# First block's attention: 64-wide heads turned in pairs and 32-wide index heads in fours, scores from row groups into different banks

## The chip, the core and the metric

The kernel runs on one core of one Trainium2 chip. The metric is device time in microseconds of one execution. Five engines work from queues of their own: TensorE (PE; its weight loads are PEld), VectorE (DVE), ScalarE (ACT), GpSimd (POOL) and SyncE (SP), which issues nearly all DMAs. They meet at semaphores only.

## The reference

Two transformer blocks one after the other, batch 1, 256 tokens, width 1024, each of depth 2. The change is in the mixer of the first block, of which this is what matters:

```python
u = x @ w_in                       # 3400 columns, split:
a_cq, a_ckv, a_kpe, b_q, b_k, b_v, b_qi, b_ki, b_wi, c_qkv = split(u)
# a: 8 heads, keys 96 wide (64 + 32 rotary), values 64 wide
s = einsum('bqhd,bkhd->bhqk', q, k) * 96 ** -0.5; s = where(causal, s, -1e30)
o_a = softmax(s) @ v
# b: sparse attention. 8 index heads of 32 share one key; 4 heads of 64 share one key and value
rel = relu(einsum('bqhd,bsd->bqhs', rope(qi), rope(ki)))
score = where(causal, einsum('bqhs,bqh->bqs', rel, wi) * scale, -1e30)
sel = top_k(score, 64)             # o_b: softmax over the selected keys only
# c: 3 x 4 dilated-window heads of 64 with keys and values of their own,
#    joined by the softmax of their log-sum-exps
o = concat([o_a, o_b, o_c]) @ w_o
```

After it come a residual with layer norm and a mixture of experts (top 2 of 8 in one of 4 groups). The second block has a GLA mixer and an SSD mixer.

## The kernel before

`block1` runs the first block's two layers as a loop of two passes over all engines. Tokens lie on partitions in two tiles of 128 (`TT` = 2, index t); t = 1 attends to 256 keys, t = 0 to 128. A pass has the input projection (`project`, L604) into `U`, the latents' projections into `QM`, `KM` and `VM` (`dense`, L501), the indexer, the attention loop, the output projection, the router and the experts.

*Turns.* Heads lie along the free axis, and a score product contracts over the head's width, which must lie on partitions. So `turn` (L494) transposes each head's 128 tokens by a product with the identity into a PSUM bank, four heads to a bank, and ScalarE copies the bank (`copy`, L847) to `QT`, `KTt`, `QIT` or `KIT`. A 64-wide head fills partitions 0 to 63 only, a 32-wide one 0 to 31.

*Indexer* (the prefix of the attention). 18 turns (`qiT`, `kiT`), five copies, 16 products (L780) of 32 rows into six banks (`rel`), six copies with Relu to `REL0` (t = 0) and `REL` (t = 1), from which VectorE sums the index scores (`index_sums`, L1282) and later picks the top 64 (`index_best`, MAX8 and MATCH_REPLACE8).

*Attention loop.* Six groups g of four heads: 0 and 1 are the 96-wide ones, 2 to 4 the dilated, 5 the sparse one. With the two token tiles that makes twelve units, u = 2g + t. In turn u TensorE does, in this order: the turns of the next group (even u only, `group_turns`), the turns of the probabilities of u (`prob_turns`), the scores of unit u + 2 (`scores`, L551), one chunk of the second block's conditioning product (`ada_chunk`, L586: 32 columns of weights in each of four strips of the array) and the outputs of u (`outputs`, L573). VectorE softens unit u + 2 (`soften`: scale and mask L1116, maximum L1121, negation L1123), takes out the conditioning row (L1311) and the outputs, and between them does its index sums and top-k rounds in units 0 to 6. ScalarE copies the next group (`group_copies`), then the turned probabilities, then exponentiates unit u + 1 (L951). Units 0 and 1 are scored ahead of the loop.

*Banks.* PSUM's eight banks are handed out in rotation by `plan_block1`, in the order in which TensorE fills them: a fill waits until what stood in that bank, eight keys earlier, has been read (`claim`), a reader until it is filled (`filled`), and each write and each read is counted on a semaphore of its bank.

*Weights of the conditioning product.* SyncE loads chunk u, 2.1 MB in two halves, into one of three places (`HALVES`; one half lies in `QIT`, whose owner must be through: it waits for `("rel", 1, 3)`), chunk u + 3 when chunk u's product is done (L393). After the loop, at `o_ready`, it starts on the expert weights.

## Time and profile before

| | us |
|---|---|
| three timed runs | 2290.03, 2293.17 (median), 2296.86 |
| the profiled execution | 2284.75 |
| its span in the trace | 2283.2 |
| TensorE busy | 2053.2 (90%) |
| VectorE busy | 1204.2 (53%) |
| ScalarE busy | 726.9 (32%) |

Times in the trace are counted from the start of the span. Pass 0 of the layer loop has its indexer and attention loop at 114 to 209 us, pass 1 at 609 to 703. The page's chain of what ended last reaches back only to about 1028 us, the second block, so that the attention stage is read from timelines and windows. A TensorE row's duration includes the latency to PSUM of the last pass; the pace of a train of passes is read from start to start.

### The profile page before, as it was taken

The numbers are of one execution on the slowest core, as the hardware profiler recorded it, in microseconds if no ns is written. First come the engines' busy times: TensorE is split into PE (matmuls) and PEld (weight loads), VectorE is DVE, ScalarE is ACT, GpSimd is POOL, SyncE is SP. The second block draws the span as 40 slices with busy tenths as digits, with TensorE's granted clock in tenths as the row PEclk, the third lists the DMA queues.
The fourth block names the chain that finished last, engine by engine and source line by source line (L and its number), as shares of the span: only waits on it lengthen the run. The fifth ranks groups of instructions, "written<-read, shape, count | busy, mean of one in ns | idle before, by whom it ended". The sixth has DMA issues, their size and how long they took to land.

```text
span 2283.2 us, 32536 instructions
## 1 busy us (share of the span) xinstructions
PE 2053.2 (90%) x12086; PEld 1459.1 (64%) x12086; DVE 1204.2 (53%) x2131; ACT 726.9 (32%) x1317; POOL 167.6 (7%) x155
## 2 busy tenths in 40 slices
PE   6999888879999878868998999999979988998997
PEld 4777533326785423325886788888868776756896
DVE  3364411124373311136558586666666876845766
ACT  3453200114452100015334311111154436623332
POOL 2001100001002000005421100000000000000000
PEclk9999999999999989998999999999999998999999
DMA  7569699984589799961322232322212342333552
GB/s 219 186 235 342 218 409 408 396 320 140 192 286 313 280 357 396 397 261 48 111 74 74 93 129 74 111 107 78 82 65 75 130 145 95 130 106 138 211 185 99
DMA packets 151935, 440.38 MB, mean 193 GB/s; under 512 B 10368, under 2 KB 12848, under 8 KB 143456
## 3 DMA queue, kind: packets, MB, share of 16 engines
q1 hardware_dynamic: 142704, 412.72, 48.5%
q0 software_dynamic: 8352, 22.39, 3.4%
q10 hardware_dynamic: 720, 3.15, 0.3%
q8 instruction: 101, 1.65, 0.3%
q14 instruction: 58, 0.48, 0.1%
HBM read 534.52 MB, written 1.21 MB: 235 GB/s over the span
## 4 chain that ended last, share of the span: by engine, by line
PE 40%; DVE 6%; ACT 4%; DVEq 2%; issue 1%; DMA 1%; ACTq 0%; POOL 0%; SPq 0%; POOLq 0%
PE bank L2113 25%; PE bank L2204 11%; PE bank L2255 4%; DVE ARENA L3223 1%; ACT ARENA L2765 1%; PE bank L2118 1%; ACT UT L2536 0%; DVEq L2839 0%; ACTq L2539 0%; DVE XA L2840 0%; DVEq L3225 0%; DMA W<-in_ffn_w 0%; ACT ARENA L2758 0%; DVE WLO L3164 0%; ACT ARENA L2513 0%
## 5 line engine op out<-in xcount | busy, mean ns | idle before, releaser
L2549 ACT ACTIVATE WPH<-W 128x1024 fp32r<-128x1024 f32 x128 | 135.5, 1063 | 400.2 <-PE bank L2113 200.2
L2113 PE MATMUL bank<-UH,WPH 128*128 128x512 f32 (+1 forms) x512 | 174.2, 340 | 6.1 <-DVE UL L2847 2.7
L2113 PE MATMUL bank<-UL,WPH 128*128 128x512 f32 (+1 forms) x512 | 173.1, 338 | 0.0
L2113 PE MATMUL bank<-UH,WPL 128*128 128x512 f32 (+1 forms) x512 | 172.8, 338 | 0.0
L2885 DVE TENSOR_TENSOR WPL<-W,WPH 128x1024 fp32r<-128x1024 f32 x128 | 153.5, 1220 | 17.2 <-ACT WPH L2549 17.2
L2204 PE MATMUL bank<-WPH,MHH 128*128 128x512 f32 x384 | 149.8, 390 | 0.0
L2204 PE MATMUL bank<-WPL,MHH 128*128 128x512 f32 x384 | 149.5, 389 | 0.0
L2204 PE MATMUL bank<-WPH,MHL 128*128 128x512 f32 x384 | 149.4, 389 | 0.0
L1438 DVE TENSOR_TENSOR H<-SG,bank 128x256 f32<-128x256 f32 x24 | 10.1, 422 | 238.7 <-ACT SG L1014 238.7
L2113 PE MATMUL bank<-ARENA 128*128 128x64 f32 (+4 forms) x528 | 107.1, 363 | 19.4 <-DVEq L3263 7.8
L704 PE MATMUL bank<-WC,H 128*32 128x512 f32 x768 | 95.1, 639 | 28.6 <-DMA WC<-in_expert_w_down 24.1
L667 PE MATMUL bank<-W,XG 128*32 128x512 f32 x768 | 90.8, 614 | 24.9 <-DMA W<-in_expert_w_up 12.4
L2113 PEld LDWEIGHTS bank<-UH,WPH 128*128 128x128 f32 x512 | 97.8, 191 | 19.1 <-issue 3.6
L2113 PEld LDWEIGHTS bank<-ARENA 128*128 128x128 f32 (+1 forms) x528 | 81.9, 208 | 39.4 <-issue 19.3
L2113 PEld LDWEIGHTS bank<-UL,WPH 128*128 128x128 f32 x512 | 97.9, 191 | 10.4
L2113 PEld LDWEIGHTS bank<-UH,WPL 128*128 128x128 f32 x512 | 97.8, 191 | 10.2
L2113 PE MATMUL bank<-XHI,PHI 128*128 128x512 f32 (+2 forms) x264 | 100.0, 379 | 4.2 <-DVE XLO L2847 2.4
L667 PE MATMUL bank<-WA,XG 128*32 128x512 f32 x768 | 90.7, 614 | 13.0 <-DMA WA<-in_expert_w_up 13.0
L501 PE MATMUL bank<-W,XT 128*128 128x512 f32 x192 | 88.2, 619 | 11.7 <-DMA W<-in_w_in 7.0
L2113 PE MATMUL bank<-XHI,WLO 128*128 128x512 f32 (+2 forms) x264 | 97.2, 368 | 0.0
L2113 PE MATMUL bank<-XLO,PHI 128*128 128x512 f32 (+2 forms) x264 | 96.8, 367 | 0.0
L1014 ACT ACTIVATE SG<-bank 128x256 f32<-128x256 f32 x24 | 9.2, 384 | 263.9 <-issue 139.8
(449 smaller groups left out, 4249.9 us busy)
## 6 DMA issues: line engine op xcount, KB each, us to landing
WC<-in_expert_w_down SPq DMA_DIRECT2D x32, 2048.0 KB
W<-in_ffn_w SPq DMA_DIRECT2D x64, 1024.0 KB, 6.2
W<-in_ada_w SPq DMA_DIRECT2D x32, 1024.0 KB, 6.8
WA<-in_expert_w_gate SPq DMA_DIRECT2D x16, 2048.0 KB
WA<-in_expert_w_up SPq DMA_DIRECT2D x16, 2048.0 KB
W<-in_expert_w_gate SPq DMA_DIRECT2D x16, 2048.0 KB
W<-in_expert_w_up SPq DMA_DIRECT2D x16, 2048.0 KB
WC<-in_expert_w_down ACTq DMA_DIRECT2D x32, 1024.0 KB
```

Source lines behind the costliest of these rows:

```text
L501: last = nc.tensor.matmul(bank[r.bank(key)][:, 0:n], lhs[k], rhs[k], start=(k == 0), stop=(k == len(lhs) - 1))
L667: last = nc.tensor.matmul(bank[r.bank(key)][32 * g:32 * g + 32, :], xg[:, 4 * part + k, col:col + 32], WA[part][:, g, :, k, :], start=(par ...
L704: last = nc.tensor.matmul(bank[r.bank(key)][32 * g:32 * g + 32, :], H[i // MQ][:, f, 32 * g:32 * g + 32], WC[:, g, f, n * CHUNK:(n + 1) * ...
L1438: r.read_done(nc.vector.tensor_tensor(H[q // MQ][:], SG[q // MQ][:].rearrange("p (n f) -> p f n", f=2), bank[r.bank(key)][:, EH:2 * EH].re ...
L2113: return nc.tensor.matmul(bank[r.bank(key)][0:rows, cols[0]:cols[1]], lhs, rhs, start=start, stop=stop)
L2118: return nc.tensor.transpose(bank[r.bank(key)][0:m, j * P:j * P + k], src, ident[0:k, 0:k])
L2204: last = nc.tensor.matmul(bank[r.bank(key)][:, :], a, x[:, k, :], start=first and k == 0 and z == 0, stop=last_block and kp == 1 and k == ...
L2255: last = nc.tensor.matmul(bank[r.bank(key)][:, :], x[:, kk, tok], a[:, k, :], start=kp == 0 and k == 0 and z == 0, stop=kp == 3 and k == 1 ...
L2549: nc.scalar.activation(piece_view(WPH, q), piece_src(i, q), ACT.Copy).then_inc(hi_done, 1)
L2765: last = nc.scalar.activation(SEGD[:, jt, z, h, :], SEGD[:, jt, z, h, :], ACT.Exp, bias=NCUM[:, jt, col:col + 1])
L2885: nc.vector.tensor_tensor(piece_view(WPL, q), piece_src(i, q), piece_view(WPH, q).bitcast(F32), ALU.subtract).then_inc(lo_done, 1)
L3223: last = nc.vector.scalar_tensor_tensor(acc, src, CW[:, m, k:k + 1], acc, ALU.mult, ALU.add)
```

## The change

Sizes and sums stay; the layout of the turned heads, the order of the products and the banks change.

- A turn takes 128 columns: two neighbouring 64-wide heads, or four 32-wide ones. Head 2i + j of a group comes to lie on partition half j, slot i, and index head 4i + j on quarter j, slot i. Groups 2 to 4 have 8 turns in 2 banks instead of 16 in 4, group 5 6 in 2 instead of 10 in 3, the indexer 6 in 3 instead of 18 in 5. Groups 0 and 1 stay as they are.
- Where one key serves several heads it must lie on every half or quarter: a new tile `KREP` takes it, written by two VectorE copies and one more drain ahead of `rope_b`.
- A score product reads the rows of its half or quarter, and half j writes bank j of the unit. Both halves' first heads come first, then both second heads. So a unit at t = 0 has two banks instead of one, and the indexer's t = 0 four instead of two; ScalarE makes eight `rel` copies (four of 256 columns and four of 512) instead of six of 512, and VectorE softens t = 0 of groups 2 to 5 in two operations of two heads.
- `plan_block1` lists the new keys in the new order.

```diff
--- before.py
+++ after.py
@@ -135,6 +135,18 @@
         ins.then_inc(self.empty[self.at[key][0]], 1)
 
 
+def score_banks(u):
+
+    return 2 if u >= 4 else u % 2 + 1
+
+
+def score_heads(u, j):
+
+    if u >= 4:
+        return slice(j, 4, 2)
+    return slice(0, 4) if u % 2 == 0 else slice(2 * j, 2 * j + 2)
+
+
 def plan_block1(full, empty):
     r = Ring(full, empty)
     keys = []
@@ -144,16 +156,16 @@
     keys += [("cT", t) for t in range(TT)]
     keys += [("q", n, t) for n in range(2) for t in range(TT)]
     keys += [("kv", n, t) for n in range(2) for t in range(TT)]
-    keys += [("qiT", t, h) for t in range(TT) for h in range(2)] + [("kiT",)]
-    keys += [("rel", 0, j) for j in range(2)] + [("rel", 1, j) for j in range(4)]
+    keys += [("qiT", t) for t in range(TT)] + [("kiT",)]
+    keys += [("rel", t, j) for t in range(TT) for j in range(4)]
     for u in range(-2, 12):
         g2, t2 = divmod(u + 2, 2)
         if u < 10 and t2 == 0:
-            keys += [("qT", g2, 0), ("qT", g2, 1), ("kT", g2, 0)] + ([("kT", g2, 1)] if g2 < 5 else [])
+            keys += [(what, g2, i) for what in ("qT", "kT") for i in range(2 if g2 < 2 else 1)]
         if u >= 0:
             keys += [("pT", u, j) for j in range(u % 2 + 1)]
         if u < 10:
-            keys += [("s", u + 2, j) for j in range(t2 + 1)]
+            keys += [("s", u + 2, j) for j in range(score_banks(u + 2))]
         if u >= 0:
             keys += [("ada", u), ("o", u)]
     keys += [("oT", t, h) for t in range(TT) for h in range(2)]
@@ -237,7 +249,7 @@
             WDH0 = low.enter_context(nc.sbuf_tensor("WDH0", [P, KT, CHUNK], F32R))
         REL = sb("REL", [P, IDX_H, SEQ])
         QIT = sb("QIT", [P, IDX_H, SEQ])
-        KIT = sb("KIT", [IDX_D, SEQ])
+        KIT = sb("KIT", [P, SEQ])
         DMASK = sb("DMASK", [P, 3 * P])
 
         REL0 = PT[:].rearrange("p s h n -> p (s h n)")[:, 0:IDX_H * P].rearrange("p (h n) -> p h n", h=IDX_H)
@@ -251,6 +263,7 @@
         CQT = sb("CQT", [P, 3, SEQ])
         O = sb("O", [P, TT, D])
         AROW = sb("AROW", [P, 12, P])
+        KREP = sb("KREP", [P, TT, 2, P])
         place[0].close()
 
         place[0] = ctx
@@ -503,13 +516,15 @@
                 r.fill_done(last, key)
 
             def group_src(g, h, t, what):
-                if g < 2:
-                    hh = 4 * g + h
-                    return QM[:, t, hh * QH:(hh + 1) * QH] if what == "q" else KM[:, t, hh, :]
+                hh = 4 * g + h
+                return QM[:, t, hh * QH:(hh + 1) * QH] if what == "q" else KM[:, t, hh, :]
+
+            def pair_src(g, i, t, what):
+
                 if g < 5:
-                    c0 = C_DIL + ((g - 2) * 4 + h) * HD + (DIL_COLS if what == "k" else 0)
-                    return U[:, t, c0:c0 + HD]
-                return U[:, t, C_BQ + h * HD:C_BQ + (h + 1) * HD] if what == "q" else U[:, t, C_BK:C_BK + HD]
+                    c0 = C_DIL + (g - 2) * 4 * HD + i * P + (DIL_COLS if what == "k" else 0)
+                    return U[:, t, c0:c0 + P]
+                return U[:, t, C_BQ + i * P:C_BQ + (i + 1) * P] if what == "q" else KREP[:, t, 1, :]
 
             def values(g, h, k):
                 if g < 2:
@@ -525,32 +540,40 @@
                     r.read(pe, ("kv", 1, 1), l)
                 if g == 2:
                     pe.wait_ge(rope_c, l + 1)
-                for t in range(TT):
-                    turn(l, ("qT", g, t), [group_src(g, h, t, "q") for h in range(4)])
-                if g < 5:
+                if g < 2:
+                    for t in range(TT):
+                        turn(l, ("qT", g, t), [group_src(g, h, t, "q") for h in range(4)])
                     for t in range(TT):
                         turn(l, ("kT", g, t), [group_src(g, h, t, "k") for h in range(4)])
                 else:
-                    turn(l, ("kT", g, 0), [group_src(g, 0, t, "k") for t in range(TT)])
+                    turn(l, ("qT", g, 0), [pair_src(g, i, t, "q") for i in range(2) for t in range(TT)])
+                    turn(l, ("kT", g, 0), [pair_src(g, i, t, "k") for i in range(2 if g < 5 else 1) for t in range(TT)])
 
             def scores(l, u):
                 g, t = divmod(u, 2)
-                dd = QH if g < 2 else HD
-                r.read(pe, ("qT", g, 1), l)
-                r.read(pe, ("qT", g, 0), l)
-                r.read(pe, ("kT", g, 0), l)
-                if g < 5:
-                    r.read(pe, ("kT", g, 1), l)
-                n = (t + 1) * P
+                for what in ("qT", "kT"):
+                    for i in range(2 if g < 2 else 1):
+                        r.read(pe, (what, g, i), l)
+                n, tok = (t + 1) * P, slice(t * P, (t + 1) * P)
+                if g >= 2:
+                    for j in range(2):
+                        r.claim(pe, ("s", u, j), l)
+                    for i in range(2):
+                        for j in range(2):
+                            key, rows = ("s", u, j), slice(j * HD, (j + 1) * HD)
+                            last = nc.tensor.matmul(bank[r.bank(key)][:, i * n:(i + 1) * n], QT[rows, g % 2, i, tok],
+                                                    KTt[rows, g % 2, i if g < 5 else 0, 0:n], start=True, stop=True)
+                            if i == 1:
+                                r.fill_done(last, key)
+                    return
                 per = 4 if t == 0 else 2
                 for j in range(t + 1):
                     key = ("s", u, j)
                     r.claim(pe, key, l)
                     for i in range(per):
                         h = j * per + i
-                        last = nc.tensor.matmul(bank[r.bank(key)][:, i * n:(i + 1) * n],
-                                                QT[0:dd, g % 2, h, t * P:(t + 1) * P],
-                                                KTt[0:dd, g % 2, h if g < 5 else 0, 0:n], start=True, stop=True)
+                        last = nc.tensor.matmul(bank[r.bank(key)][:, i * n:(i + 1) * n], QT[0:QH, g % 2, h, tok],
+                                                KTt[0:QH, g % 2, h, 0:n], start=True, stop=True)
                     r.fill_done(last, key)
 
             def prob_turns(l, u):
@@ -763,23 +786,22 @@
 
                 pe.wait_ge(rope_b, l + 1)
                 for t in range(TT):
-                    for h in range(2):
-                        turn(l, ("qiT", t, h), [U[:, t, C_QI + (4 * h + j) * IDX_D:C_QI + (4 * h + j + 1) * IDX_D] for j in range(4)])
-                turn(l, ("kiT",), [U[:, t, C_KI:C_KI + IDX_D] for t in range(TT)])
+                    turn(l, ("qiT", t), [U[:, t, C_QI + i * P:C_QI + (i + 1) * P] for i in range(2)])
+                turn(l, ("kiT",), [KREP[:, t, 0, :] for t in range(TT)])
                 for t in range(TT):
-                    for h in range(2):
-                        r.read(pe, ("qiT", t, h), l)
+                    r.read(pe, ("qiT", t), l)
                 r.read(pe, ("kiT",), l)
                 for t in range(TT):
-                    n = (t + 1) * P
-                    per = 4 if t == 0 else 2
-                    for j in range(IDX_H // per):
-                        key = ("rel", t, j)
-                        r.claim(pe, key, l)
-                        for i in range(per):
-                            last = nc.tensor.matmul(bank[r.bank(key)][:, i * n:(i + 1) * n],
-                                                    QIT[0:IDX_D, j * per + i, t * P:(t + 1) * P], KIT[:, 0:n], start=True, stop=True)
-                        r.fill_done(last, key)
+                    n, tok = (t + 1) * P, slice(t * P, (t + 1) * P)
+                    for j in range(4):
+                        r.claim(pe, ("rel", t, j), l)
+                    for i in range(2):
+                        for j in range(4):
+                            key, quarter = ("rel", t, j), slice(j * IDX_D, (j + 1) * IDX_D)
+                            last = nc.tensor.matmul(bank[r.bank(key)][:, i * n:(i + 1) * n], QIT[quarter, i, tok], KIT[quarter, 0:n],
+                                                    start=True, stop=True)
+                            if i == 1:
+                                r.fill_done(last, key)
 
                 group_turns(l, 0)
                 scores(l, 0)
@@ -854,19 +876,17 @@
                              bank[r.bank(key)][:, :].rearrange("p (k n) -> p k n", k=4))
 
             def group_copies(l, g):
-                dd = QH if g < 2 else HD
                 for what, dst in (("qT", QT), ("kT", KTt)):
-                    for t in range(TT):
-                        key = (what, g, t)
-                        if key not in r.at:
-                            continue
-                        if g >= 2 and what == "qT" and t == 0:
+                    for i in range(2 if g < 2 else 1):
+                        key = (what, g, i)
+                        if g >= 2 and what == "qT":
                             r.filled(act, ("s", 2 * (g - 2) + 1, 1), l)
-                        if what == "kT" and g == 5:
-                            copy(l, key, dst[0:dd, g % 2, 0, :], bank[r.bank(key)][0:dd, 0:SEQ])
+                        if g < 2:
+                            copy(l, key, dst[0:QH, g % 2, :, i * P:(i + 1) * P],
+                                 bank[r.bank(key)][0:QH, :].rearrange("p (h n) -> p h n", h=4))
                         else:
-                            copy(l, key, dst[0:dd, g % 2, :, t * P:(t + 1) * P],
-                                 bank[r.bank(key)][0:dd, :].rearrange("p (h n) -> p h n", h=4))
+                            m = 1 if what == "kT" and g == 5 else 2
+                            copy(l, key, dst[:, g % 2, 0:m, :], bank[r.bank(key)][:, 0:m * SEQ].rearrange("p (i n) -> p i n", i=m))
 
             def gathered(l, j, half):
 
@@ -930,18 +950,15 @@
                         r.read_done(nc.scalar.activation(
                             VM[:, t, 256 * n:256 * n + 256].rearrange("p (h d) -> p h d", h=4), b[:, :, NOPE:], ACT.Copy), key)
                 for t in range(TT):
-                    for h in range(2):
-                        key = ("qiT", t, h)
-                        copy(l, key, QIT[0:IDX_D, 4 * h:4 * h + 4, t * P:(t + 1) * P],
-                             bank[r.bank(key)][0:IDX_D, :].rearrange("p (h n) -> p h n", h=4))
-                copy(l, ("kiT",), KIT[:], bank[r.bank(("kiT",))][0:IDX_D, 0:SEQ])
+                    key = ("qiT", t)
+                    copy(l, key, QIT[:, 0:2, t * P:(t + 1) * P], bank[r.bank(key)][:, 0:SEQ].rearrange("p (i n) -> p i n", i=2))
+                copy(l, ("kiT",), KIT[:], bank[r.bank(("kiT",))][:, 0:SEQ])
                 for t in range(TT):
                     n = (t + 1) * P
-                    per = 4 if t == 0 else 2
-                    for j in range(IDX_H // per):
+                    for j in range(4):
                         key = ("rel", t, j)
-                        copy(l, key, (REL0, REL)[t][:, j * per:(j + 1) * per, 0:n],
-                             bank[r.bank(key)][:, 0:per * n].rearrange("p (h n) -> p h n", h=per), ACT.Relu)
+                        copy(l, key, (REL0, REL)[t][:, j:IDX_H:4, 0:n],
+                             bank[r.bank(key)][:, 0:2 * n].rearrange("p (h n) -> p h n", h=2), ACT.Relu)
                 group_copies(l, 0)
 
                 def weights_of(u):
@@ -1105,16 +1122,16 @@
 
                 g, t = divmod(u, 2)
                 n = (t + 1) * P
-                per = 4 if t == 0 else 2
                 m0 = 0 if t == 0 else P
                 mask = (DMASK if g == 5 else MASK[:, (0, 0, 1, 2, 3)[g], :])[:, m0:m0 + n]
                 if u >= 3:
                     r.filled(v, ("pT", u - 3, (u - 3) % 2), l)
-                for j in range(t + 1):
+                per = 2 if score_banks(u) == 2 else 4
+                for j in range(score_banks(u)):
                     key = ("s", u, j)
                     r.filled(v, key, l)
                     r.read_done(nc.vector.scalar_tensor_tensor(
-                        PR[:, u % 3, j * per:(j + 1) * per, 0:n],
+                        PR[:, u % 3, score_heads(u, j), 0:n],
                         bank[r.bank(key)][:, 0:per * n].rearrange("p (h n) -> p h n", h=per),
                         (QH if g < 2 else HD) ** -0.5, bc(mask, 1, per), ALU.mult, ALU.add), key)
                 v.drain()
@@ -1257,6 +1274,9 @@
                 rope(U[:, :, C_QI:C_WI].rearrange("p t (h d) -> p t h d", d=IDX_D), 9, HALF_I, HALF_M + HALF_H)
                 nc.vector.tensor_scalar(U[:, :, C_WI:C_DIL], U[:, :, C_WI:C_DIL], IDX_D ** -0.5 * IDX_H ** -0.5, None, ALU.mult)
                 nc.vector.tensor_copy(KM[:, :, :, NOPE:QH], bc(U[:, :, C_KPE:C_KPE + ROPE], 2, MLA_H))
+                v.drain()
+                for i, (c0, dd) in enumerate(((C_KI, IDX_D), (C_BK, HD))):
+                    nc.vector.tensor_copy(KREP[:, :, i, :].rearrange("p t (m d) -> p t m d", d=dd), bc(U[:, :, c0:c0 + dd], 2, P // dd))
                 v.drain().then_inc(rope_b, 1)
                 for n in range(5, N_IN):
                     low_weights(n)
@@ -1275,10 +1295,9 @@
 
                 def index_sums(t, h0, h1):
                     sc, mask, n = index_span(t)
-                    per = 4 if t == 0 else 2
                     for h in range(h0, h1):
-                        if h % per == 0:
-                            r.read(v, ("rel", t, h // per), l)
+                        if h < 4:
+                            r.read(v, ("rel", t, h), l)
                         nc.vector.scalar_tensor_tensor(sc, (REL0, REL)[t][:, h, 0:n], U[:, t, C_WI + h:C_WI + h + 1],
                                                        mask if h == 0 else sc, ALU.mult, ALU.add)
                         v.drain()
```

## Rows read from the trace of the kernel before

**Rows 1.** The head of the page: span and number of instructions.
```profile
span 2283.2 us, 32536 instructions
```

**Rows 2.** Windows, pass 0: stretch, length, busy us (count) by engine, clock, DMA, GB/s.
```profile
117.00:129.00 12.00, 10.55 (x48) 8.58 (x48) 3.49 (x10) 6.72 (x13) 0.00 (x0) 0.72 0.68 239
...
145.00:165.00 20.00, 19.16 (x297) 17.38 (x300) 16.57 (x54) 11.61 (x36) 0.00 (x0) 1.00 0.94 343
```

**Rows 3.** Windows, pass 1, same columns.
```profile
617.00:629.00 12.00, 11.12 (x49) 9.20 (x48) 3.60 (x7) 6.89 (x17) 0.00 (x0) 0.58 0.27 88
```

**Rows 4.** TensorE, timeline, pass 0, prefix: start, lasting, engine, line, out<-in, shape, count.
```profile
114.85 2.13 PE L494 MATMUL bank<-ident,U 128*32 128x128 f32 x18
117.92 6.97 PE L780 MATMUL bank<-KIT,QIT 32*128 32x128 f32 x32 [0.95 <-ACT KIT L847]
...
129.36 2.86 PE L551 MATMUL bank<-KTt,QT 96*128 96x128 f32 x16 [0.88 <-ACT KTt L847]
...
137.00 1.96 PE L586 MATMUL bank<-W,cond 128*32 128x128 f32 x64
```

**Rows 5.** Timeline of all engines, pass 0, prefix: ScalarE's copies, same columns.
```profile
115.59 2.02 ACT L847 ACTIVATE QIT<-bank 32x512 f32<-32x512 f32 x4
...
117.50 0.38 ACT L847 ACTIVATE KIT<-bank 32x256 f32<-32x256 f32 x1
...
119.11 0.60 ACT L847 ACTIVATE PT<-bank 128x512 f32<-128x512 f32 x1 [1.24 <-PE bank L780]
...
120.01 0.60 ACT L847 ACTIVATE PT<-bank 128x512 f32<-128x512 f32 x1 [0.30 <-PE bank L780]
...
120.87 0.60 ACT L847 ACTIVATE REL<-bank 128x512 f32<-128x512 f32 x1 [0.27 <-PE bank L780]
121.74 0.60 ACT L847 ACTIVATE REL<-bank 128x512 f32<-128x512 f32 x1 [0.27 <-PE bank L780]
```

**Rows 6.** Timeline of TensorE, pass 0, loop, units 5 to 8.
```profile
166.21 1.04 PE L494 MATMUL bank<-ident,PR 128*128 128x128 f32 x8
...
172.82 1.91 PE L494 MATMUL bank<-ident,U 128*64 128x128 f32 x16
174.57 0.60 PE L494 MATMUL bank<-ident,PR 128*128 128x128 f32 x4
175.74 1.15 PE L551 MATMUL bank<-KTt,QT 64*128 64x128 f32 x8 [0.56 <-ACT KTt L847]
176.81 1.95 PE L586 MATMUL bank<-W,cond 128*32 128x128 f32 x64
178.70 1.10 PE L573 MATMUL bank<-U,PT 128*128 128x64 f32 x8
...
180.61 1.99 PE L551 MATMUL bank<-KTt,QT 64*128 64x256 f32 x8
182.53 1.08 PE L586 MATMUL bank<-XT,cond 128*32 128x128 f32 x32
```

**Rows 7.** Timeline of TensorE, pass 1, prefix.
```profile
612.27 6.39 PE L780 MATMUL bank<-KIT,QIT 32*128 32x128 f32 x32 [0.95 <-ACT KIT L847]
...
623.12 4.73 PE L551 MATMUL bank<-KTt,QT 96*128 96x128 f32 x16 [0.88 <-ACT KTt L847]
...
631.68 1.96 PE L586 MATMUL bank<-W,cond 128*32 128x128 f32 x64
```

**Rows 8.** Timeline of VectorE, pass 0, input projection.
```profile
84.82 4.64 DVE L1221 TENSOR_TENSOR WLO<-W,WDH 128x1024 fp32r<-128x1024 f32 x4 [3.69 <-ACT WDH L899]
```

**Rows 9.** Timeline of VectorE, pass 0, loop, softening of unit 5.
```profile
159.31 1.29 DVE L1116 SCALAR_TENSOR_TENSOR PR<-bank,MASK 128x512 f32<-128x512 f32 x2 [0.17 <-issue]
...
161.98 0.17 DVE L1123 TENSOR_SCALAR MX<-MX 128x4 f32<-128x4 f32 x1
```

**Rows 10.** Timeline of ScalarE, pass 0, loop: last exponential of unit 5.
```profile
164.01 0.51 ACT L951 ACTIVATE PR<-PR,MX 128x256 f32<-128x256 f32 x1
```

**Rows 11.** DMA of 130 to 208 in 40 equal slices: GB/s of each.
```profile
GB/s 0 0 0 0 8 150 399 353 346 398 398 129 255 411 383 310 406 371 57 312 405 348 338 406 303 47 367 401 313 382 404 267 208 382 360 325 393 400 327 390
```

## Prediction

> **What bounds the kernel now.** I read the page first [rows 1]: 2283.2 us of span, one core. The change touches only the attention stage of the first block, which runs once in each of two passes of the layer loop, so I went to the windows of that stage. In pass 0 [rows 2] TensorE is busy 10.55 of 12 us in the short prefix (117 to 129, clock 0.72, so part of it was granted 1.2 GHz and not 2.4) and about 19 of 20 us in the loop over twelve units (clock 1.00). VectorE is busy 16.57 of 20 us there and the DMA engines are at 0.94. In pass 1 [rows 3] the prefix has clock 0.58. So the loop is TensorE's, but VectorE and DMA stand close behind: a saving on TensorE is worth its size only until one of them comes last. Everything after the loop hangs on `o_ready` (SyncE waits for it before the expert weights, TensorE before the mixing product), so what the stage loses, the span loses one for one.
>
> **How products and turns are paced.** An fp32 product stands in the trace as two passes. Eight passes of 128 columns lie between the first two relevance copies, 120.01 - 119.11 = 0.90 us, 0.112 us a pass; four of 256 columns between the next two, 121.74 - 120.87 = 0.87, 0.217 us [rows 5]. These use 32 rows of the array and are no faster than others. Scores of a 64-wide group take 1.07 us at t = 0 (175.74 to 176.81) and 1.92 at t = 1 (180.61 to 182.53), 16 turns 1.75 (172.82 to 174.57), 0.109 each [rows 6]. 32 passes that go to four different 32-column strips last 1.08 from 182.53 with some 0.27 of latency at the end (0.29 by (b) below), 0.026 each [rows 6]: strips of columns do run side by side, four for one. Strips of rows are never used side by side in this trace, so the price of the new products has to be bounded: at best 0.112/2 and 0.217/2 a pass with 64 rows and a quarter of them with 32, at worst the paces above plus a change of strip, for which the difference between 8 x 0.112 = 0.90 and the 1.07 above (0.17 for a change in and one out, some 0.1 each) is the nearest row.
>
> There is a middle: the eight passes of L573, only 64 moving columns wide, last 1.10 from 178.70 with the same latency, (1.10 - 0.27) / 7 = 0.118 each [rows 6], as long as 128 columns. There the load of 128 weight columns sets the pace. If such loads into different strips queue up, passes of 128 columns gain nothing and those of 256 go from 0.217 to 0.112. I take the best case, since the column strips of the trace show loads as well as products of four strips overlapping; the others are rivals. The Trainium skill ("TensorE: Matmul & The Clock Gate", LDWEIGHTS) says that a load's time goes by its columns and not its rows: the trace agrees (L573), and by this rule alone the middle case would hold. Its Part 3 gives 3.07x for four row tiles at 512 columns; no row here shows it, and by that factor the best case would lose about a quarter of its gain in the index products.
>
> **Part 1, the prefix.** Before, in pass 0 [rows 4, 5]: turns from 114.85, ScalarE's four QIT copies from 115.59 (0.48 apart) and the KIT copy at 117.50, products from 117.92, first copy 119.11, scores from 129.36. After:
> (a) 6 turns for 18. ScalarE is free at 115.59, so the turns saved (12 x 0.109 = 1.3) are mostly hidden behind it; but it now makes two copies of 256 columns and KIT's (0.38 lasting, about 0.28 apart) and is through at 115.59 + 2 x 0.28 + 0.38 = 116.53. Products start at 116.57, 1.35 earlier.
> (b) Products: four passes in each strip of rows, 4 x 0.112 = 0.45 for t = 0 and 4 x 0.217 = 0.87 for t = 1, where they took 6.9 us to 124.83. First copy: 116.57 + 0.45 + 0.3 (latency, 119.11 - 117.92 - 0.90) + 0.1 = 117.4.
> (c) ScalarE now comes last: four copies of 256 columns, 0.28 apart (1.1; two of 512 before), four of 512, 0.5 apart (2.0), the four group copies, 3 x 0.49 + 0.59 (2.1): 117.4 + 5.2 = 122.6. The 16 turns of group 0, unchanged, end by 116.57 + 1.4 + 3.5 = 121.5 even at 1.2 GHz (twice 1.75), so they lie beside it. Scores from 122.65 against 129.36: 6.7 us. The same steps in pass 1, where 612.27 to 623.12 = 10.85 us lie between product and scores [rows 7], give 1.35 + 10.85 - 6.1 = 6.1.
> (d) The clock. From first scores to the first conditioning chunk it is 7.64 us in pass 0 at 2.4 GHz (129.36 to 137.00 [rows 4]) and 8.56 in pass 1, partly at 1.2 (623.12 to 631.68 [rows 7]). TensorE will stand idle more ahead of these scores, so I take pass 1's 8.56 for both (-0.9 in pass 0) and another 1.0 in each, between 0 and 3.6 (scores and 16 turns at half pace: 1.75 + 1.9 more).
> (e) VectorE's index sums (about 3.3 us) start with the first copy and end by 121.2, before it is wanted. The two KREP copies and the drain, about 0.8 us, fall into the 3.69 us in which VectorE waits for ScalarE before 84.82 [rows 8]: nothing; uncovered they would cost 0.8. SyncE waits for ("rel", 1, 3) with one load, issued earlier now: nothing.
> Prefix: 6.7 - 0.9 - 1.0 + 6.1 - 1.0 = 9.9 us for both passes.
>
> **Part 2, the loop, groups 2 to 5.** (f) Turns: 8 for 16 in groups 2 to 4, 6 for 10 in group 5. From the first turn to the scores it is 2.92 us (172.82 to 175.74 [rows 6]), because the scores wait for the last of four copies. With two: turned at 0.87 + 0.27, the second copy starts at 1.22, ends at 1.81, scores at 1.85: 1.05 each. Group 5, which has 4 turns and one copy fewer to save, about 0.45 (4 x 0.109 by the turns). (g) Scores: 4 x 0.112 = 0.45 at t = 0 and 4 x 0.217 = 0.87 at t = 1 saved, 5.3 for four groups. Together 3.6 + 5.3 = 8.9 a pass on TensorE's own count.
> (h) VectorE takes some back. Its queue holds mask, softmax and top-k rounds in program order; through units 3 and 4 it never waits for TensorE. Its last operation of softening unit 5 starts at 161.98 [rows 9], then ScalarE's exponentials, the last from 164.01, 0.51 long with a readout behind it [rows 10], then unit 5's turn on TensorE, at 166.21 [rows 6]. That turn can move to 164.65 at the earliest, 1.56 us, where TensorE would gain 1.05 x 2 + 0.45 x 2 + 0.87 = 3.9. So 2.3 are lost there; after it TensorE is last again (s7 0.87, turns 1.05, s8 0.45, s9 0.87, turns 0.45, s10 0.45, s11 0.87 = 5.0). Softening a t = 0 unit from two banks adds one operation's overhead, some 0.09. Net 1.56 + 5.0 - 0.1 = 6.5 a pass, 13.0 for both. The bank order makes ("s", u + 4, 1) wait for ("s", u + 3, 0) to be read; that read starts at 159.31 [rows 9], within the same bound.
>
> **Sum.** 9.9 + 13.0 = 22.9 us. Against the profiled execution's own 2284.75 that is 2261.9; that execution lies 8.4 below the median of the timed runs (2293.17), to which I apply the sum: 2270.3, taken as 2270.
>
> **Rivals.**
> *Loads queue (middle case).* 16 passes at t = 0 take 1.8 and the first copy comes at 118.1: prefix 0.6 less a pass. The loop keeps f, loses the 0.45s: 5.5 a pass. 8.5 + 11.1 = 19.6: 2273.5.
> *No overlap of row strips at all.* For it: nothing in the trace shows any. The turns and copies still go: prefix about 2.5 a pass after the clock, loop 1.56 + 1.05 + 0.45 = 3.1. 11 us: 2282. If each change of strip also costs the 0.1 above (3 to 7 in a unit's scores, 15 in the index products, some 3.9 a pass) it is 3 us: 2290.
> *The conditioning weights become the bound.* Nine chunks of 2.1 MB are loaded in the loop, each when the one three units earlier is used. In the slices they run at up to 411 GB/s, mostly 310 to 406 [rows 11], 5.3 us a chunk; TensorE uses one every 6.6 now, every 5.5 after. At the 343 GB/s of the window [rows 2] a chunk takes 6.1 and the last lands just as it is wanted; at 332, the mean of the slices from the first full one on [rows 11], it takes 6.3 and the last comes 1.5 us late, at 300 it takes 7.0 and comes 7 late. I take 3.5 a pass between them: 2277.
> *The clock falls in the loop (the slower side).* TensorE now waits for VectorE in places where it had none, and packed products are fewer. Against it: clock 1.00 with 64-row products and packed strips of columns. A stretch T at 1.2 GHz costs up to T/2; it decides beyond 46 us of the two loops' some 126. At half of them, 63 us: +31 - 23 = +8, 2301.
>
> **How the numbers follow.** Best case 0.50, queued loads 0.20, no overlap 0.10, with costly changes 0.05, DMA 0.08, clock 0.04, something larger than I count 0.03. Predicted is the likeliest, 2270. The range reaches up through "no overlap" (2282) with the spread of the runs, 2286, and down to 2257, where the clock costs nothing (2 + 0.9), VectorE's hold is half of mine (2) and the runs come out as the profiled one did (8.4). The bound of what this kernel's timing can tell from no change is 0.3%, 6.9 us: faster 0.88 (the first three, DMA and the larger, less 0.03 of the plain no-overlap case, whose 11 us are nearest to the bound), same 0.08 (those 0.03 and the costly changes), slower 0.04 (the clock).
>
> **What the changed profile would show.** First relevance copy about 2.6 us and not 4.3 after the first index turn; scores of group 0 about 6 us after the first index product (11 before). Passes of L780's line starting in fours (best), every 0.112 (queued) or as before (no overlap). Scores of groups 2 to 5 in some 0.6 and 1.05 us. VectorE busier in the loop, and TensorE waiting for ScalarE's exponentials before the turn of unit 5. I am wrong if the group-0 scores start less than 3 us earlier, if TensorE waits for `ada_w` loads, or if clock digits in the loop are under 1.

## The result, and the profile after

The changed kernel takes 2264.27 us (median of 6 runs, 2259.13 to 2268.83) against 2289.32 for the kernel before beside it (2280.28 to 2296.86). The ratio is 0.9895, 95% interval 0.988 to 0.9909: 1.05% or 25 us faster. The profiled execution is the 2259.13 one, with a span of 2257.6 against 2283.2 [rows 1].

```profile
span 2257.6 us, 32346 instructions
```

Windows of the same stretches as [rows 2, 3] (stretch, length, busy us and count of TensorE's products, its weight loads, VectorE, ScalarE, GpSimd, then clock, DMA share, GB/s):

```profile
117.00:129.00 12.00, 9.28 (x78) 7.91 (x79) 7.13 (x16) 8.81 (x23) 0.00 (x0) 0.86 0.70 259
145.00:165.00 20.00, 17.82 (x300) 15.62 (x295) 16.77 (x56) 9.12 (x31) 0.00 (x0) 1.00 0.98 341
...
597.00:609.00 12.00, 8.84 (x74) 7.59 (x75) 7.85 (x17) 8.87 (x23) 0.00 (x0) 0.86 0.74 263
```

In the prefix TensorE is no longer nearly full (9.28 of 12 us where it was 10.55) and its clock is better, not worse: 0.86 for 0.72 and 0.58. In the loop TensorE fell from 19.16 to 17.82 of 20 us: now it waits there. The clock stays 1.00.

TensorE in the prefix of pass 0, which answers to [rows 4] (start, lasting, engine, line, out<-in, shape, count, idle time before it and its releaser):

```profile
115.12 0.60 PE L507 MATMUL bank<-ident,U 128*128 128x128 f32 x4
115.56 0.38 PE L507 MATMUL bank<-ident,KREP 128*128 128x128 f32 x2
117.14 1.59 PE L801 MATMUL bank<-KIT,QIT 32*128 32x128 f32 x32 [1.20 <-ACT KIT L869]
118.66 1.08 PE L507 MATMUL bank<-ident,QM 128*96 128x128 f32 x8
119.57 1.04 PE L507 MATMUL bank<-ident,KM 128*96 128x128 f32 x8
123.19 4.52 PE L575 MATMUL bank<-KTt,QT 96*128 96x128 f32 x16 [2.58 <-ACT KTt L869]
```

The 32 passes of the index products last 1.59 us; they lasted 6.97 [rows 4]. Then TensorE is through with its turns at 120.6 and stands idle for 2.58 us until ScalarE has copied. ScalarE in the same stretch, which answers to [rows 5]:

```profile
115.86 0.67 ACT L869 ACTIVATE QIT<-bank 128x256 f32<-128x256 f32 x2
116.39 0.41 ACT L869 ACTIVATE KIT<-bank 128x256 f32<-128x256 f32 x1
117.85 1.21 ACT L869 ACTIVATE PT<-bank 128x256 f32<-128x256 f32 x4 [1.04 <-PE bank L801]
118.92 2.10 ACT L869 ACTIVATE REL<-bank 128x512 f32<-128x512 f32 x4
120.83 1.13 ACT L869 ACTIVATE QT<-bank 96x512 f32<-96x512 f32 x2
121.79 1.15 ACT L869 ACTIVATE KTt<-bank 96x512 f32<-96x512 f32 x2
```

From 117.85 to the end of the KTt copies ScalarE has no gap: it is the engine that comes last, as the forecast said.

TensorE in the loop of pass 0, units 4 to 8, which answers to [rows 6]:

```profile
142.52 0.71 PE L564 MATMUL bank<-KTt,QT 64*128 64x128 f32 x8 [0.38 <-ACT KTt L869]
143.17 1.08 PE L609 MATMUL bank<-W,cond 128*32 128x128 f32 x32
...
146.97 1.14 PE L564 MATMUL bank<-KTt,QT 64*128 64x256 f32 x8
148.03 1.96 PE L609 MATMUL bank<-W,cond 128*32 128x128 f32 x64
...
154.70 0.71 PE L564 MATMUL bank<-KTt,QT 64*128 64x128 f32 x8 [1.47 <-DVE PR L1133]
...
159.05 1.07 PE L507 MATMUL bank<-ident,PR 128*128 128x128 f32 x8 [0.72 <-ACT PR L968]
...
164.83 1.04 PE L507 MATMUL bank<-ident,U 128*128 128x128 f32 x8
...
166.62 0.71 PE L564 MATMUL bank<-KTt,QT 64*128 64x128 f32 x8 [0.30 <-ACT KTt L869]
```

Scores take 0.65 us at t = 0 (142.52 to 143.17) and 1.06 at t = 1 (146.97 to 148.03), where they took 1.07 and 1.92 [rows 6]. Two waits are new: the scores of unit 6 wait 1.47 us for VectorE to read unit 5's banks, and the turn of unit 5 waits 0.72 us for its exponentials. Pass 1 has the same two, 1.46 and 0.72.

The stage by its marks, in both kernels (each mark is the start of a group in TensorE's timeline; us):

| stretch | before, pass 0 / 1 | after, pass 0 / 1 | gained | forecast |
|---|---|---|---|---|
| first index turn to first index product | 3.08 / 3.08 | 2.02 / 2.02 | 1.06 + 1.06 | 1.35 + 1.35 |
| to group-0 scores | 11.43 / 10.85 | 6.06 / 6.05 | 5.37 + 4.80 | 5.35 + 4.75 |
| to first conditioning chunk | 7.65 / 8.56 | 8.23 / 8.17 | -0.58 + 0.39 | -1.9 - 1.0 |
| to the turn of O | 71.75 / 71.74 | 65.67 / 65.44 | 6.08 + 6.30 | 6.5 + 6.5 |
| sum | 93.91 / 94.23 | 81.97 / 81.68 | 24.5 | 22.9 |

Of the 25.6 us of the span 24.5 lie in this stage. The rest of the kernel varies by itself: from the turn of O in pass 0 to the first index turn in pass 1, of which the kernels here change nothing but the two KREP copies, it is 400.4 us before, 398.5 after, and 397.4 to 403.9 in others. So single spans say little about steps of 1 to 4 us. The marks of the prefix repeat to a few hundredths where the clock is the same, those of the loop mostly to 0.1 to 0.3 (65.38 to 65.67 in six passes of the same loop code), and below I read those first.

Part of the gain comes through the clock: the stage has 17.1 us at 1.2 GHz before (6.8 + 10.2) and 6.8 after (3.4 + 3.4). At half pace 17.1 us cost at most 8.5, and the 6.8 cost 1.1 (8.23 and 8.17 us from scores to first chunk, where it is 7.64 at 2.4 GHz). So at most some 7 of the 24.5 us came this way, an estimate. No run separates them.

### The profile page after: what moved, and what is told of

Same layout as the page of the kernel before. It is cut to its first block, busy times and chain, and to the rows that moved or that the text cites. A ratio compares the mean times of both kernels' runs of the same rounds, so it can differ in the third digit from the quotient of the medians.

```text
span 2257.6 us, 32346 instructions
## 1 busy us (share of the span) xinstructions
PE 2023.1 (90%) x12006; PEld 1433.2 (63%) x12006; DVE 1204.8 (53%) x2143; ACT 718.2 (32%) x1303; POOL 167.7 (7%) x155
## 4 chain that ended last, share of the span: by engine, by line
PE 40%; DVE 7%; ACT 4%; DVEq 2%; issue 1%; DMA 1%; ACTq 0%; POOL 0%; SPq 0%; POOLq 0%
PE bank L2132 25%; PE bank L2223 11%; PE bank L2274 4%; DVE ARENA L3242 1%; ACT ARENA L2784 1%; PE bank L2137 1%; DVEq L2858 0%; ACT UT L2555 0%; ACTq L2558 0%; DMA W<-in_ffn_w 0%; DVE XA L2859 0%; ACT ARENA L2777 0%; DVE WLO L3183 0%; DVEq L2913 0%; DVE MHL L2924 0%
```

## The experiments

**Do the strips overlap because the program interleaves them?** The passes of each strip were put together, instead of going from strip to strip:

```diff
-                    for i in range(2):
-                        for j in range(2):
+                    for j in range(2):
+                        for i in range(2):
...
-                    for i in range(2):
-                        for j in range(4):
+                    for j in range(4):
+                        for i in range(2):
```

> The changed kernel with the two product loops exchanged (strip outside, head inside), so that all passes of one strip of rows come before those of the next. Turns, copies, banks and numbers of instructions stay. Theory (passes in different strips run side by side, and this order is what lets them): scores go back from about 0.65 and 1.06 us to 1.05 and 1.9, the index products from 1.5 to some 5.3 us; group-0 scores 6.1 -> about 8 us after the first index product, 9.5 if the clock falls; in the loop nothing is lost before unit 5, where the hold of VectorE (2.2 us) covers 0.43 + 0.86 + 0.43, and 3.4 us a pass behind it. 10 to 14 us in all over the changed kernel, about 2276. Rival (wide turns and fewer copies bring nearly all, overlap little): at most 3 us over the changed kernel.

Measured: 2265.71 us, ratio 0.9899 (0.9872 to 0.9925), as the changed kernel. My expectation missed, and the trace says how:

```profile
116.66 1.71 PE L801 MATMUL bank<-KIT,QIT 32*128 32x128 f32 x32 [1.20 <-ACT KIT L869]
118.29 0.97 PE L507 MATMUL bank<-ident,QM 128*96 128x128 f32 x7
```

The 32 passes last 1.71 for 1.59. In the records of the single passes the first four start at 116.656, .669, .686 and .700, and the passes that signal the four banks, each the last of its strip at t = 0, start at 117.063, .106, .119 and .136. The signals themselves, which are events and not modelled ends, come 0.69, 0.75, 0.81 and 0.87 us after the first start. Had the strips been worked one after another, each bank would have been signalled 0.45 us (4 x 0.112) before the next; had passes only been held to start in their order, still some 0.34 (3 x 0.112). So a pass for another strip does not wait for the ones before it in the source. (The trace doesn't show in which order the compiled program holds them; that it kept the source's order is taken, not shown.) This kernel therefore did not take the overlap away and can't price it. The Trainium skill ("TensorE: Matmul & The Clock Gate", Part 3, The mechanism) says that MATMULs start strictly in the order of the program; the start times recorded here differ from that if the compiled program kept the source's order, and by the 0.34 us above a strict order would have made this kernel slower (an estimate).

**What is the overlap worth?** First attempt: the same order, and a drain of TensorE behind each strip (`pe.drain()` after the strip's last pass, 24 a pass of the layer loop), with a control that has as many drains at the same places in the kernel before, where nothing overlaps.

> The changed kernel with the passes of one strip of rows issued together and a drain of TensorE behind each strip (8 a pass in the index products, 16 in the scores of groups 2 to 5), so that no two strips can run side by side. Theory (strips of rows run beside each other whatever the program's order, and that is most of the gain of the new products): index products last 5.3 us or more and not 1.3, scores 0.9 to 1.1 at t = 0 and 1.8 to 2.0 at t = 1 where they are 0.72 and 1.14; of the 5.3 + 5.3 us of TensorE's time a pass that come back, some 1.8 in the prefix (ScalarE covers the rest) and 3.5 in the loop (the hold of unit 5 covers the rest) reach the end: 10.6 us for both passes over the changed kernel, and on top what the drains cost (0 to 0.27 each, 0 to 13 us; the control with the same drains in the kernel before says how much). Rival (the gain lies in fewer turns and copies, the overlap is worth little): no more over the changed kernel than the control is over the kernel before.

> Control: the kernel before with a drain of TensorE after every two products of the index products and of the scores of groups 2 to 5, as many drains at the same places as in the kernel with its strips kept apart. Nothing overlaps here in any case, so what it costs over the kernel before is the drains' own price: 48 drains in both passes, between 0 and 0.27 us each (the latency behind a last product), so 0 to 13 us; I take 0.1 each, 5 us.

Measured: strips kept apart 2301.73 us, ratio 1.0051 (1.0032 to 1.0069); the control 2307.22, ratio 1.0078 (1.0059 to 1.0097), both slower than the kernel before. The control missed its forecast of 5 us: it lost 18. In its loop 16 drains cost 5.35 us (77.10 for 71.75), 0.33 each and not 0.1, and in the prefix of pass 0 it had 13.7 us of 1.2 GHz, where the kernel before had 6.8. In the loop the two can be set against each other: 74.06 - 65.67 = 8.4 us a pass over the changed kernel less the control's 5.35 leaves 3.0 (3.2 in pass 1) against a forecast of 3.5, if a drain costs the same in both kernels. In the prefix they can't: with the strips apart the index products and the scores behind them lie in 17.1 and 20.5 us of 1.2 GHz. So the loop speaks for the overlap, and the prefix stayed open.

Second attempt, without drains: as many products, over all rows of the array (the heads are no longer kept apart, so the values are not the reference's).

```diff
-                            key, rows = ("s", u, j), slice(j * HD, (j + 1) * HD)
+                            key, rows = ("s", u, j), slice(0, P)
...
-                            key, quarter = ("rel", t, j), slice(j * IDX_D, (j + 1) * IDX_D)
+                            key, quarter = ("rel", t, j), slice(0, P)
```

> The changed kernel with its index products and the scores of groups 2 to 5 over all 128 rows of the array and not over a quarter or half of them: same turns, copies, banks, order and number of products, no drains, but no strips of rows (so the heads are not kept apart, and these products are not the reference's). Theory (strips of rows side by side are what makes the new products cheap): index products last 5.3 us (16 x 0.112 + 16 x 0.217) and not 1.22; ScalarE's copies then end later, and group-0 scores come some 8.2 us after the first index product and not 6.06 (+2.1); the loop becomes 3.5 us a pass longer (0.45 or 0.87 for each unit's scores, those of units 4 to 6 inside VectorE's hold); 11 us in all over the changed kernel, near 2275. Rival (what the kernel with drains lost came from drains and clock, strips are worth little): within 3 us of the changed kernel.

Measured: 2274.54 us, ratio 0.9932 (0.9904 to 0.9959); by the marks 88.02 + 86.39 = 174.4 us against 163.65, 10.8 more where 11 were expected.

```profile
117.12 5.48 PE L801 MATMUL bank<-KIT,QIT 128*128 128x128 f32 x32 [1.20 <-ACT KIT L869]
122.44 1.04 PE L507 MATMUL bank<-ident,QM 128*96 128x128 f32 x8
...
125.59 2.86 PE L575 MATMUL bank<-KTt,QT 96*128 96x128 f32 x16 [1.24 <-ACT KTt L869]
...
133.24 3.43 PE L609 MATMUL bank<-W,cond 128*32 128x128 f32 x64
```

From the first start to the last of the 32 index passes it is 5.10 us here and 1.22 in the changed kernel, a ratio of 4.2. That overstates it, because the last pass of each strip runs on behind the last start: up to the signal of the last bank it is 5.49 and 1.69 us, 3.3 times with the latency in both, and with one pass of 0.217 added to each it is 5.3 and 1.4, 3.7 times. The group-0 scores come 8.47 us after the first product and not 6.06 (8.2 expected). The loop is 68.26 in pass 1, 2.8 over the changed kernel; in pass 0 it is 69.89, of which 1.6 are the 3.4 us at 1.2 GHz from 133.5 on (the chunk at 133.24 lasts 3.43, and 1.96 at 2.4 GHz). So the overlap is worth some 10 of the 25 us, and the theory holds. The other 13.7 by the marks are turns, copies and the clock together. The Trainium skill ("TensorE: Matmul & The Clock Gate", Part 3, Measured speedup vs the span model) has 3.07x for four row tiles at 512 columns. Here, at 128 and 256 columns of fp32, it is 3.3x up to the last signal, a little above; the starts of the changed kernel come in fours some 0.11 and 0.22 us apart, which is the full gain in pace.

**How do the two parts share the gain?** Only the indexer's part of the change (its turns, copies, products, KREP and the sums' order) was put into the kernel before, groups 2 to 5 left as they were.

> The kernel before with the indexer's part of the change alone (6 turns, 16 products in four strips, 8 banks, KREP); groups 2 to 5 as before. Theory (the two parts add up, neither is hidden): group-0 scores 6.1 us after the first index product, the loop from first conditioning chunk to the turn of O 71.7 us as before; 11.5 to 13 us under the kernel before, about 2277. Rival (an earlier start is given back in the loop, by the conditioning weights or VectorE): the loop grows by some 3 us a pass and 5 to 7 us are left.

Measured: 2278.51 us, ratio 0.9958 (0.9943 to 0.9973). Turn to product 2.02, product to scores 6.06, as in the changed kernel, and the loop 71.75 in both passes, as before. In pass 1 scores to first chunk took 9.72 with 6.8 us at 1.2 GHz, so it has less than its full share; in pass 0, at 2.4 GHz, 7.64. By the marks 11.1 us are gained over both passes and by the times 9.1, where 11.5 to 13 were expected; the rival's longer loop did not come. The parts are independent: prefix one, loop the other.

**Does VectorE hold TensorE in the loop?** The top-k rounds were left out of the changed kernel and of the kernel before (group 5 then attends to other keys than in the reference):

```diff
-                    for _ in range(rounds):
+                    for _ in range(0):
```

> The changed kernel without the 16 top-k rounds of each pass (MAX8 and MATCH_REPLACE8 left out, so group 5 attends to other keys than the reference); VectorE has some 15 us a pass less to do in units 1 to 6. Theory (VectorE holds TensorE back by 2.2 us a pass at the scores of unit 6 and the turn of unit 5): both waits go, the loop is 65.5 - 2.2 = 63.3 us, 4.4 us under the changed kernel. Rival (behind VectorE the conditioning weights come last): the waits move to the first passes of the conditioning product and under 1.5 us is gained.

> The kernel before without the 16 top-k rounds of each pass (left out as in the run beside it). Theory (before, TensorE sets the loop alone, and VectorE's full queue cost nothing): loop 71.7 us within 0.3, time within 2 us of the kernel before. Rival (VectorE already cost something before): 1 us a pass or more is gained.

Measured: in the kernel before nothing changes, 2288.84, ratio 1.0007 (0.999 to 1.0024), loop 71.74 in both passes. In the changed kernel 2260.37, ratio 0.9875 (0.9848 to 0.9903), loop 63.72 and 63.58, 1.95 and 1.86 less. The waits of the changed kernel in the loop, TensorE's view (who waits, for whom, us in total, times, longest):

```profile
PE bank L564 <- DVE PR L1133: 1.5, 1, 1.5
...
PE bank L507 <- ACT PR L968: 0.7, 1, 0.7
```

Without the rounds both lines are gone. The same VectorE work costs nothing before and 2 us a pass after, because TensorE got faster around it.

**Can that hold be taken away without leaving work out?** The same rounds were spread:

```diff
-                    if u in (1, 2):
-                        index_best(0, TOPK // 16)
-                    if 3 <= u < 7:
+                    if 1 <= u < 5:
+                        index_best(0, TOPK // 32)
+                    if 5 <= u < 9:
                         index_best(1, TOPK // 32)
-                    if u == 2:
+                    if u == 4:
                         index_mask(0)
-                    if u == 6:
+                    if u == 8:
                         index_mask(1)
```

> The changed kernel with the same top-k rounds spread over more units: two rounds behind each of units 1 to 4 for the first 128 tokens and behind each of units 5 to 8 for the second, masks behind units 4 and 8, where the changed kernel has four rounds in units 1 and 2 and two in units 3 to 6. Theory (VectorE's queue of softening and top-k rounds holds TensorE before the scores of unit 6 and the turn of unit 5, 2.19 us a pass): the hold goes in part, loop 1 to 2 us shorter a pass, 2 to 4 us in all. Rival (the rounds are only moved, and VectorE holds TensorE later, at units 6 to 9): loop as long as in the changed kernel, within 0.5 us.

Measured: 2259.73 us, ratio 0.9874 (0.9856 to 0.9892), loop 63.85 and 63.84, 1.82 and 1.60 less. The rounds fit beside TensorE's work:

```profile
153.88 0.71 PE L564 MATMUL bank<-KTt,QT 64*128 64x128 f32 x8 [0.44 <-issue]
...
157.35 1.05 PE L507 MATMUL bank<-ident,PR 128*128 128x128 f32 x8
```

The scores of unit 6 and the turn of unit 5 follow with no wait for VectorE or the exponentials (at 154.70 and 159.05 in the changed kernel). The hold was one of order, not of VectorE's total work.

**Does ScalarE's queue set the prefix?** Its four copies of group 0 were put ahead of the four relevance copies of t = 1:

```diff
                 for t in range(TT):
...
                              bank[r.bank(key)][:, 0:2 * n].rearrange("p (h n) -> p h n", h=2), ACT.Relu)
-                group_copies(l, 0)
+                    if t == 0:
+                        group_copies(l, 0)
```

> The changed kernel with ScalarE's four copies of group 0 placed ahead of the four relevance copies of the second 128 tokens. Theory (ScalarE comes last in the prefix, and the group-0 scores wait for its queue, 2.58 us at the end of pass 0): scores 1.0 to 2.0 us sooner after the first index product, 6.06 down to some 4.5, bounded then by TensorE's own turns; 2 to 4 us in all, less what VectorE's later index sums give back. Rival (TensorE's turns of group 0 come last, in part at 1.2 GHz): under 0.5 us a pass.

Measured: 2258.64 us, ratio 0.9864 (0.9846 to 0.9881). Product to scores 4.88 us for 6.06, with no stretch at 1.2 GHz in either pass (scores to chunk 7.64), loop as it was: 3.5 us in all by the marks. I had expected 4.5; the scores claim a bank that ScalarE frees with a relevance copy, and this now comes last (the row below, from the kernel with both rearrangements, has the same wait).

**Is it the idle time ahead of the group-0 scores that lowers the clock?** Three products that nobody needs were put into it (`keep_busy(("s", 0, 0), 3)` behind the group's turns).

> The changed kernel with three unneeded products of 512 columns in the 2.58 us in which TensorE stands idle ahead of the group-0 scores. Theory (that idle time is what brings a stretch of 3.4 us at 1.2 GHz behind it in some executions, 8.2 us from scores to the first conditioning chunk against 7.64 without): no stretch below 2.4 GHz between the scores and the chunk, 7.64 us in both passes, 0 to 1.1 us in all, which the times can hardly show. Rival (the products delay the scores, or the stretch at 1.2 GHz comes from something earlier): scores later than 6.1 us after the first index product, or the stretch still there.

Measured: 2264.54 us, ratio 0.9893 (0.9871 to 0.9916).

```profile
122.24 2.74 PE L634 MATMUL bank<-MASK,ident 128*128 128x512 f32 x6
124.98 2.86 PE L575 MATMUL bank<-KTt,QT 96*128 96x128 f32 x16
```

The group-0 scores last 2.86 and not 4.52, start as late as before (6.06), and scores to chunk is 7.64 in both passes. But the kernel with its strips in turn, with the same idle time, had no such stretch either (7.64 and 7.65), and the one with the spread rounds had it in one pass of two. So the same idle time goes with such a stretch in some passes and not in others; that filling it prevents the stretch is not shown by two passes. It is worth some 0.6 us a pass at most here (8.23 and 8.17 to 7.64).

**Both rearrangements together.**

> The changed kernel with both rearrangements: ScalarE's copies of group 0 ahead of the relevance copies of the second 128 tokens, and the top-k rounds two behind each of units 1 to 8. Theory (the two act at different places, each with what it gave alone: 1.2 a pass from product to scores with 0.55 of clock, 1.6 to 1.8 in the loop): stage of some 78.3 us a pass where the changed kernel has 81.8, 7 us in all, near 2257. Rival (something else, the conditioning weights or VectorE, comes last once both are gone): loop longer than 64.2 us, or TensorE waiting for ada_w.

Measured: 2256.69 us, ratio 0.9852 (0.983 to 0.9874); the marks give 78.03 and 78.25 us a pass, 7.4 less than the changed kernel in both, as expected. The loop is 63.48 and 63.69, and no wait for `ada_w` appears, though the last chunk of pass 0 now lands only 0.9 us before it is used.

```profile
123.52 2.86 PE L575 MATMUL bank<-KTt,QT 96*128 96x128 f32 x16 [1.41 <-ACT REL L869]
```

**Why did the first index product come 0.3 us later than forecast?** On the kernel with both rearrangements TensorE's four claims of banks for the first index products were put ahead of its waits for QIT and KIT:

```diff
+                for j in range(4):
+                    r.claim(pe, ("rel", 0, j), l)
                 for t in range(TT):
                     r.read(pe, ("qiT", t), l)
...
-                    for j in range(4):
+                    for j in range(4 if t else 0):
                         r.claim(pe, ("rel", t, j), l)
```

> The kernel with both rearrangements, and TensorE's four claims of banks for the first index products put ahead of its waits for the turned QIT and KIT, where they stood behind them. Theory (in the changed kernel TensorE works through four more waits of some 0.09 us each after the KIT copy has ended, 0.34 us from copy to product where it was 0.04 before, and this is the 0.3 us by which the first part of the prefix came out later than forecast): first index product 1.7 to 1.75 us after the first index turn and not 2.02, everything behind it as it was, 0.3 us a pass, 0.6 in all: near 2256, no measurable step in the times. Rival (the 0.3 us is the latency of a copy over 128 partitions or of the copy's last semaphore): 2.02 us as it was.

Measured: 2254.96 us, ratio 0.9851 (0.9828 to 0.9874), not to be told from the one before by its time, but by the trace:

```profile
114.06 0.60 PE L507 MATMUL bank<-ident,U 128*128 128x128 f32 x4
...
115.80 1.59 PE L803 MATMUL bank<-KIT,QIT 32*128 32x128 f32 x32 [0.92 <-ACT KIT L871]
```

1.74 us from turn to product in both passes, where it was 2.02. The 0.3 us were waits, each long fulfilled, that stood behind the one that counted: in the changed kernel the four claims fill three records behind the wait for KIT, at 116.937, 117.030 and 117.106.

## Why the prediction was right

The time (2264.3 for 2270) lies in the range, and both the direction and the mechanism hold. Of the 5.7 us between them 3.9 are the base: the kernel before had a median of 2293.17 in the runs shown and 2289.32 in these. The other 2 are the sum, 25.05 for 22.9 (2270.3 had been rounded to 2270). That it came so near is in part luck: the clock gave 2.7 us more than forecast, and the first part of the prefix (0.6) and the loop (0.6) less. By its steps:

(a) Turns and index copies: 1.06 a pass, not 1.35. The copies are as forecast (first at 0.74 us after the turn, KIT's end at 1.68), but the product starts 0.34 after KIT's end and not 0.04. I had taken the latency over from the kernel before, where one claim stands behind the last wait; after the change there are four, one for each bank. The kernel with early claims shows it.

(b), (g) Products four and two abreast: right. 32 index passes in 1.22 between the first start and the last, 16 x 0.112/4 + 16 x 0.217/4 = 1.3; scores 0.42 shorter at t = 0 (forecast 0.45) and 0.86 at t = 1 (0.87). Of the rivals "loads queue" is refuted by the t = 0 scores, which it would have left at 1.07, and "no overlap" by the kernel over all rows, which shows what that case would have looked like (2274.5; I had priced it at 2282 and, with costly changes of strip, at 2290: too dear, since turns, copies and the clock alone gave 13.7 us by the marks, 188.1 to 174.4, and not 11). That the overlap does not hang on the order in the source I had not thought of; the forecast did not need it. One step beside the sum was miscounted: a speedup of 3.07 in place of 4 leaves the index products 0.33 of their time and not 0.25, which loses a tenth of the gain and not a quarter.

(c) ScalarE last, group-0 scores 6.1 us after the first index product: 6.06 and 6.05. The row to see this in was the count of ScalarE's copies after the product, and moving the copies confirmed it by shifting the scores to 4.88.

(d) The clock was the term that was mis-sized. I took 8.56 + 1.0 for both passes; measured 8.23 and 8.17, with 3.4 us at 1.2 GHz each, behind 6.8 and 10.2 before. More idle time ahead of the scores did not mean more time at 1.2 GHz. I had put 2.9 us of loss in the sum, and 0.2 came (0.58 lost, 0.39 gained). That is outside my bounds, which began at 8.56: I had not allowed for the new stretch being shorter than the one in the kernel before. Why it is shorter no run shows. With it at its true size and (a) and the loop at theirs, the sum is 24.5.

(e) Hidden work: right. The two KREP copies lie in VectorE's wait, which is 3.42 us now [rows 8]:

```profile
81.18 0.50 DVE L1279 COPY KREP<-U 128x256 f32<-128x256 f32 x2
85.10 1.23 DVE L1238 TENSOR_TENSOR WLO<-W,WDH 128x1024 fp32r<-128x1024 f32 x1 [3.42 <-ACT WDH L919]
```

(f) Turns: right. From the turn to the scores it is 1.85 us in group 2 (2.72 before), 1.79 in group 4 (2.92 before) and 1.65 in group 5 (2.04 before): 0.87 and 1.13 for 1.05, 0.39 for 0.45. I had taken group 4's 2.92 for all; group 3 has the hold in it.

(h) VectorE's hold: the place, unit 5, and the size were right. Its turn gained 1.58 us against the first chunk (29.21 to 27.63) where 1.56 was forecast, and the two waits, 1.47 + 0.72 = 2.19, are the 2.3 that I had put down as lost. Behind it the terms add to 4.96 as measured, but 4.50 came through (unit 5's turn to the turn of O: 42.54 to 38.04). Some 0.34 of it are in the last wait:

```profile
197.09 0.63 PE L507 MATMUL bank<-ident,O 128*128 128x128 f32 x4 [1.95 <-DVEq L1369]
```

It was 1.61 before. That VectorE's last steps for O don't move up quite as far is only read from this row; no run tests it.

The conditioning weights did not become the bound. The last chunk lands at 189.25 and is used at 191.26, 2.0 us of slack (2.3 before, 200.93 and 203.26); in pass 1 the slack is 1.2 us (2.2 before). From unit 2 to unit 8 TensorE took a chunk every 5.9 us, not every 5.5 as I had it, while the DMA engines moved 371 GB/s from 170 to 200 where it was 326: the faster loop started the loads sooner, and they had the bandwidth. "The clock falls in the loop" is refuted by 1.00 in the windows.

## What to carry to other kernels

Products that fill only a quarter or half of the array's rows can go into different strips and banks, and then four or two of them take the time of one; this is worth doing where TensorE comes last, and only until the next engine does. Before putting a price on it, follow the queue of each other engine past the place: here ScalarE's copies bounded one half of the gain and the order of VectorE's rounds the other, and both could be freed (7.4 us more by the marks) by moving operations that were already there. Put the wait that comes last behind all other waits of its engine, for each record of a wait that stands behind it costs some 0.09 us even when it has long been fulfilled.

## What the runs showed of the hardware

- Passes for different strips of rows run side by side whether the source interleaves them or not: with each strip's passes together the 32 index passes start within 1.33 us, interleaved 1.22, over all rows 5.10. Up to the signal of the last bank it is 1.78, 1.69 and 5.49.
- A drain of TensorE in a dense stream cost 0.33 us (0.35 in pass 1), three times what I had taken, and the prefixes with drains had 10.2 to 20.5 us at 1.2 GHz.
- A fulfilled wait on TensorE costs some 0.09 us a record: four claims in three records moved away gave 0.28.
- With four strips of 32 rows the clock was no worse: the stage's time at 1.2 GHz fell from 17.1 us to 6.8 over both passes.
